# A layer whose activation transposes move from sixteen small VectorE operations to two wide VectorE operations and sixteen ScalarE copies

## The reference

```
u = rms_norm(h); z = u @ w_in               # four mixers on slices of z -> o_0..o_3
merged = sum_j sigmoid(z_merge_j) * (o_j @ w_branch[j])
h = h + merged @ w_out                      # 2048 x 2048
v = rms_norm(h)
h = h + square(relu(v @ w_up)) @ w_down     # w_up 2048 x 8192, w_down 8192 x 2048
h = h + sigmoid(h @ w_pg) * (p @ w_pp)      # 2048 x 2048
out = rms_norm(h)
```

## Time and profile before

| | us |
|---|---|
| median of 3 runs | 1621.71 (1620.98 to 1622.74) |
| the profiled execution | 1620.44 |
| its span, first to last instruction | 1618.7 |
| PE busy | 1594.5 |
| DVE busy | 1188.3 |
| ACT busy | 765.2 |

### The profile page before, as it was taken

How to read it: one execution, slowest core, us unless ns; L and a number is a source line. 1 busy time by engine, 2 the same in 40 slices (tenths; PEclk the granted TensorE clock), 3 DMA queues, 4 the chain that set the end, 5 groups by cost and what they waited for, 6 DMA issues and landing times.

```text
span 1618.7 us, 20043 instructions
## 1 busy us (share of the span) xinstructions
PE 1594.5 (99%) x7422; PEld 1305.8 (81%) x7422; DVE 1188.3 (73%) x1613; ACT 765.2 (47%) x898; POOL 0.7 (0%) x5
## 2 busy tenths in 40 slices
PE   9999999999999999999999999999999999999997
PEld 7888887778777788888878788887888788878886
DVE  6547847785988986887988845885569655888865
ACT  7444455656344454344464433453344434444455
POOL 0000000000000000000000000000000000000000
PEclk9999999999999999999999999999999999999999
DMA  9686656465666667876666566665665666655663
GB/s 326 192 290 202 184 182 182 143 181 164 208 196 182 210 207 250 284 240 235 199 182 194 192 192 192 188 200 187 192 188 186 197 192 193 187 193 182 220 198 127
DMA packets 163426, 325.32 MB, mean 201 GB/s; under 512 B 10640, under 2 KB 15888, under 8 KB 162448
## 3 DMA queue, kind: packets, MB, share of 16 engines
q1 hardware_dynamic: 163344, 324.23, 63.9%
HBM read 313.70 MB, written 10.49 MB: 200 GB/s over the span
## 4 chain that ended last, share of the span: by engine, by line
PE 91%; DVE 6%; ACT 1%; issue 1%; DMA 0%; ACTq 0%; SPq 0%
PE ps L374 29%; PE ps L375 29%; PE ps L376 29%; DVE ps L419 3%; DVE sb L357 2%; PE ps L791 1%; ACT sb L350 0%; ACT sb L1006 0%; DVE sb L405 0%; PE ps L666 0%; PE ps L719 0%; PE ps L702 0%; PE ps L390 0%; DVE sb L1412 0%; DMA sb<-in_w_mix 0%
## 5 line engine op out<-in xcount | busy, mean ns | idle before, releaser
L357 DVE TENSOR_TENSOR sb<-sb,sb 128x1024 fp32r<-128x1024 f32 x560 | 680.1, 1223 | 301.0 <-ACT sb L350 289.1
L350 ACT ACTIVATE sb<-sb 128x1024 fp32r<-128x1024 f32 x560 | 589.2, 1060 | 648.8 <-PE ps L376 626.6
L374 PE MATMUL ps<-sb,sb 128*128 128x512 f32 (+1 forms) x2224 | 869.9, 391 | 9.6 <-DVE sb L405 6.6
L375 PE MATMUL ps<-sb,sb 128*128 128x512 f32 (+1 forms) x2224 | 862.9, 388 | 0.0
L376 PE MATMUL ps<-sb,sb 128*128 128x512 f32 (+1 forms) x2224 | 862.7, 388 | 0.0
L374 PEld LDWEIGHTS ps<-sb,sb 128*128 128x128 f32 x2224 | 417.5, 188 | 103.4 <-issue 7.6
L376 PEld LDWEIGHTS ps<-sb,sb 128*128 128x128 f32 x2224 | 417.5, 188 | 86.9
L375 PEld LDWEIGHTS ps<-sb,sb 128*128 128x128 f32 x2224 | 417.7, 188 | 83.1
L419 DVE STREAM_TRANSPOSE ps<-sb 32x256 f32<-32x256 f32 x384 | 175.1, 456 | 6.4
L396 ACT ACTIVATE sb<-ps 128x1024 fp32r<-128x1024 f32 x26 | 26.6, 1025 | 64.6 <-DVE ps L419 64.6
L1672 DVE TENSOR_TENSOR sb<-sb 128x1024 f32<-128x1024 f32 x16 | 19.6, 1226 | 25.7 <-ACT sb L1113 25.7
(11 more groups left out here) (239 smaller groups left out, 483.2 us busy)
## 6 DMA issues: line engine op xcount, KB each, us to landing
sb<-in_w_in SPq DMA_DIRECT2D x128, 512.0 KB, 4.0
sb<-in_w_up SPq DMA_DIRECT2D x128, 512.0 KB, 3.9
sb<-in_w_down SPq DMA_DIRECT2D x128, 512.0 KB, 4.3
sb<-in_w_mix SPq DMA_DIRECT2D x64, 512.0 KB, 4.1
sb<-in_w_branch SPq DMA_DIRECT2D x32, 512.0 KB, 5.5
sb<-in_w_out SPq DMA_DIRECT2D x32, 512.0 KB, 4.5
sb<-in_w_pg SPq DMA_DIRECT2D x32, 512.0 KB, 3.7
gate_mem<-sb SPq DMA_DIRECT2D x16, 512.0 KB, 5.1
```

Source lines behind the costliest of these rows:

```text
L350: act.activation(whi[:, j % RING, :], raw[:, j % RING, :], ACT.Copy).then_inc(hi_done, 1)
L357: eng.tensor_tensor(wlo[:, j % RING, :], raw[:, j % RING, :], whi[:, j % RING, :].bitcast(F32), ALU.subtract).then_inc(lo_done, 1)
L374: pe.matmul(o, xh, w_h, start=first and k == 0, stop=False)
L375: pe.matmul(o, xh, w_l, start=False, stop=False)
```

## The change

`blocks` on DVE is replaced by two steps. `strips` on DVE takes two transposes, one for each token tile, over all 128 partitions and 512 elements: each 32x32 block is transposed and stays in its strip of 32 partitions. They write to `aux[1 - par]`, the other PSUM tensor, in step 0 of the group, right behind the split of that step. Then ACT makes the sixteen moves between strips as copies from `aux[1 - par]` to `aux[par]` in the new `blocks`, 32 partitions by 256 elements each, in steps 1 to 3 (`turned`), the first of which waits for the semaphore `strips_done`. `quad_hi` and `quad_lo` stay in step 4. The transposes of the mixers' quads on PE are not touched.

```diff
-        def blocks(v, par, src, lo, hi):
-
+        def strips(v, par, src):
+
+            for tt in range(TT):
+                dst = aux[1 - par][:, :].rearrange("p (r t k n) -> p t k r n", r=4, t=TT, k=4)[:, tt]
+                ins = v.transpose(dst, src(tt).rearrange("p (k r m) -> p k r m", k=4, r=4))
+            ins.then_inc(strips_done, 1)
+
+        def blocks(act, n, par, lo, hi):
+
+            if lo == 0:
+                act.wait_ge(strips_done, n + 1)
             for i in range(lo, hi):
                 q, r = i // 4, i % 4
                 dst = aux[par][32 * r:32 * r + 32, :].rearrange("p (k t m) -> p t k m", k=4, t=TT)[:, :, :, 32 * q:32 * q + 32]
-                ins = v.transpose(dst, src[32 * q:32 * q + 32, :, :, 32 * r:32 * r + 32])
+                src = aux[1 - par][32 * q:32 * q + 32, r * S:(r + 1) * S].rearrange("p (t k m) -> p t k m", t=TT, k=4)
+                ins = act.activation(dst, src, ACT.Copy)
             if hi == 16:
                 ins.then_inc(tp_in, 1)
...
+            def turned(j, n, par):
+
+                if 1 <= j <= 3:
+                    blocks(act, n, par, (0, 5, 10)[j - 1], (5, 10, 16)[j - 1])
+
...
                         split_hi(act, u, j + AHEAD)
+                        if first and n == 0:
+                            turned(j, NCH - 1, (TP_H + NCH - 1) % 2)
+                        if 1 <= n <= NCH:
+                            turned(j, g * NCH + (TP_FF - TP_H + n - 1), (TP_FF + n - 1) % 2)
...
-            def turn(j, par, src):
-
-                if 1 <= j <= 3:
-                    blocks(v, par, src, (0, 5, 10)[j - 1], (5, 10, 16)[j - 1])
...
+            def turn_h(k, tp):
+
+                strips(v, (tp + k) % 2, lambda tt: h[:, tt, k * C:(k + 1) * C])
...
-                        if 1 <= n <= NCH:
-                            if j == 1:
-                                v.wait_ge(sg["sq_done"], g * NCH + n)
-                            turn(j, (TP_FF + n - 1) % 2, relu[(n - 1) % 2].rearrange("p (t k f) -> p t k f", t=TT, k=4))
...
+                        if 1 <= n <= NCH and j == 0:
+                            v.wait_ge(sg["sq_done"], g * NCH + n)
+                            strips(v, (TP_FF + n - 1) % 2, lambda tt: relu[(n - 1) % 2][:, tt * C:(tt + 1) * C])
```

More of the change, by code:

```diff
@@ L272, in hybrid_layer @@
         tp_hi = sem("tp_hi")
+        strips_done = sem("strips_done")
         tp_lo = sem("tp_lo")
@@ L1085, in _ @@
                         merged_hi(NCH - 1)
+                    if n:
+                        turned(j, n - 1, (TP_H + n - 1) % 2)
                     if n and j == 4:
@@ L1093, in mlp_group @@
                         split_hi(act, u, j + AHEAD)
+                        if first and n == 0:
+                            turned(j, NCH - 1, (TP_H + NCH - 1) % 2)
+                        if 1 <= n <= NCH:
+                            turned(j, g * NCH + (TP_FF - TP_H + n - 1), (TP_FF + n - 1) % 2)
+                        if final and n > NCH:
+                            turned(j, TP_P - TP_H + n - NCH - 1, (TP_P + n - NCH - 1) % 2)
                         if j == 4 and 1 <= n <= NCH:
@@ L1131, in _ @@
                     split_hi(act, U_PG + n, j + AHEAD)
+                    if n == 0:
+                        turned(j, TP_P - TP_H + NCH - 1, (TP_P + NCH - 1) % 2)
                     if n == 0 and j == 4:
@@ L1608, in _ @@
                 v.sem_inc(sg["merged_done"], 1)
-            def turn(j, par, src):
-                if 1 <= j <= 3:
-                    blocks(v, par, src, (0, 5, 10)[j - 1], (5, 10, 16)[j - 1])
-            def turn_h(j, k, tp):
-                turn(j, (tp + k) % 2, h[:, :, k * C:(k + 1) * C].rearrange("p t (k f) -> p t k f", k=4))
+            def turn_h(k, tp):
+                strips(v, (tp + k) % 2, lambda tt: h[:, tt, k * C:(k + 1) * C])
             def add_residual(n, par):
@@ L1629, in _ @@
                         merged_lo(NCH - 1)
-                    if n and j == 1:
+                    if n and j == 0:
                         v.wait_ge(grp_free, 2 * (G_WO + n))
-                    if n:
-                        turn_h(j, n - 1, TP_H)
+                        turn_h(n - 1, TP_H)
                     if n and j == 4:
@@ L1645, in mlp_group @@
                         split_lo(v, u, j + AHEAD)
-                        if first and n == 0:
-                            if j == 1:
-                                v.wait_ge(grp_free, 2 * (G_WO + NCH))
-                            turn_h(j, NCH - 1, TP_H)
-                        if 1 <= n <= NCH:
-                            if j == 1:
-                                v.wait_ge(sg["sq_done"], g * NCH + n)
-                            turn(j, (TP_FF + n - 1) % 2, relu[(n - 1) % 2].rearrange("p (t k f) -> p t k f", t=TT, k=4))
[L1654 to L1657, removed]
+                        if first and n == 0 and j == 0:
+                            v.wait_ge(grp_free, 2 * (G_WO + NCH))
+                            turn_h(NCH - 1, TP_H)
+                        if 1 <= n <= NCH and j == 0:
+                            v.wait_ge(sg["sq_done"], g * NCH + n)
+                            strips(v, (TP_FF + n - 1) % 2, lambda tt: relu[(n - 1) % 2][:, tt * C:(tt + 1) * C])
+                        if final and n > NCH and j == 0:
+                            v.wait_ge(grp_free, 2 * (G_PG - NCH + n - NCH))
+                            turn_h(n - NCH - 1, TP_P)
                         if j == 4 and 1 <= n <= NCH:
@@ L1691, in _ @@
                     split_lo(v, U_PG + n, j + AHEAD)
-                    if n == 0 and j == 1:
+                    if n == 0 and j == 0:
                         v.wait_ge(grp_free, 2 * G_PG)
-                    if n == 0:
-                        turn_h(j, NCH - 1, TP_P)
+                        turn_h(NCH - 1, TP_P)
                     if n == 0 and j == 4:
```

## The result

| | before | after |
|---|---|---|
| median of 4 runs, us | 1621.35 (1620.57 to 1622.74) | 1611.05 (1610.59 to 1612.04) |
| span of the profiled execution, us | 1618.7 | 1609.2 |

What follows compares the result with a forecast made beforehand. PE, busy 1594.5 of 1618.7 us, was taken as the bound, so only its stalls could be won: 5 x 1.6 + 2.5 = 10.5 us, and 1621.7 - 10.5 = 1611.2 us, range 1610.0 to 1619.5.

Steps and rivals of the forecast that it cites:

- six stalls: PE's waits for quad_lo ahead of tile 6: five costing 1.6 us each and one 2.5, together 10.5 us.
- The likeliest case: All stalls gone, -10.5 us, giving 1611.2 us (1610.2 to 1612.2); chance 0.60.
- c: Step from one of ACT's sixteen strip copies to the next; taken as 0.28 us.
- step 6: Took 0.28 us a copy from the 0.26 row: sixteen take 4.5 us, quad done a microsecond ahead of its deadline.
- natural place: Earliest start of ACT's split of tile 7 that PE allows, 1091.51 us in the MLP quad; forecast about 0.7 behind it.
- the partial case: Copies not overlapping, c between 0.342 and 0.42: only part of the stalls won, gain 7.6 us, 1614.1 us; chance 0.18.
- steps 1 and 2: DVE's strip transposes: 0.72 us each if strips run in parallel, starting 1.25 behind the split of tile 3, ending at 1085.79.
- step 3: ACT's sixteen copies with splits of tiles 5 and 6 among them, 0.93 us a split, before the split of tile 7.
- step 4: Quad done 3.47 us behind the start of split 7, which must start by 1093.16, so sixteen copies may take 5.48 us.
- What costs nothing: The other 18 quads, asked for later, and ACT's added 107 us of 853 idle; PE's list, SP's and DMAs unchanged.
- the slower one: Copies of 0.5 us or more make ACT the bound, each further 0.01 us costing 1 us; 1627 us at 0.52; chance 0.09.

Runs made afterwards that it cites:

- extra_8: Changed kernel with eight more ScalarE copies, which nobody reads, behind the sixteen of each quad: 1637.69 us, ratio 1.0094.
- extra_3: Changed kernel with three more ScalarE copies, which nobody reads, behind the sixteen of each quad: 1618.06 us, ratio 0.9966.
- copies_stay: Changed kernel with each of the sixteen copies kept in its own strip of partitions, so blocks land in wrong places: 1610.7 us, one run.
- copies_in_halves: Changed kernel with each of the sixteen copies made as two of 128 elements, same strips read and written: 1615.9 us, one run.
- strips_late: Changed kernel with the two strip transposes one step later, behind the split of tile 4: 1622.66 us, ratio 0.9995.
- before_by_target: Kernel before with its sixteen VectorE transposes reordered, four sources for one target strip, then the next target: 1620.93 us, ratio 0.9992.

## Why the prediction was right

The forecast was 1611.2 us and all six stalls gone; measured 1611.05. Its account of the gain held: a ceiling of 10.5 us from six stalls (10.4 by the starts), none of it outside the six quads, and the deadline for the split of tile 7. The likeliest case came out, but with no room where a microsecond was forecast, and partly by luck; that is worth reading by its terms. Counted from the start of the relu in front of the group (1080.63 before, 1077.16 after), in us:

| | forecast | measured |
|---|---|---|
| strips end | 5.16 | 4.88 |
| from there to the split of tile 7 | 6.37 | 7.73 |
| split of tile 7 | 11.53 | 12.61 |
| latest without a stall | 12.53 | 12.5 to 12.6 |

- *The value of c* (step 6) was off: 0.28 taken, 0.36 measured. The row it was read from, 0.26 behind the mixer's copy, is of operations on all 128 partitions, and such copies do come 0.27 apart from PSUM to PSUM too; the sixteen change their strip at each copy. By the prediction's own sum c = 0.36 is past the limit of 0.342 and belongs to the partial case, 16 x 0.018 = 0.29 us of stall in each MLP group. So the mechanism of that rival, a copy that does not overlap its neighbour, is the one that was measured, and the reason for setting it aside (260.85 to 261.11) did not hold. The split of tile 7 came 1.7 us behind its natural place, where 0.7 was given.
- *Strips* (steps 1 and 2): 0.70 us each as forecast (0.72), which only the parallel case gives; it fits the 32x32 array per bank of which the Trainium skill, "VectorE: DVE Perf Modes", section "The three transpose paths", tells. But the two overlap (1.31 for the pair, not 1.46), and start 1.13 behind the split, not 1.25: the row for the 1.25 is of a transpose to another strip than the last one written. Together 0.28 us earlier, just what c had used up.
- *Copies* (step 3): a split among the copies takes 1.07 us where 0.93 was counted, since the copy behind it starts at another strip of PSUM than the copy in front of it; the split behind the last copy of a batch starts 0.28 behind it, as an overlapped one, where c was counted. The two nearly cancel.
- *Deadline* (step 4): right to 0.1 us. The delay that came was 0.06.
- *What costs nothing*: right. The eighteen other quads and DVE's relief moved the span by 0.7 us at most.
- *The rivals*: the slower one, ACT as the bound from 0.5 us a copy on, has the sign that `extra_8` gave, whose copies come to (5.6 + 3.1) / 16 = 0.54 us for each of the sixteen. Its price was too low: the rival's sum gives 1629 us at 0.54, and 1637.7 was measured, and among what it left out are the late starts of two groups and the slow matmuls.

So the middle of the forecast was right by errors of opposite sign, and that is luck. The range up to 1619.5 was not too wide: 1.25 us more on the chain, in `extra_3`, took back 6.8 of the 9.5 us.

The overlap of about 93 ns between ACTIVATEs that the Trainium skill gives ("ScalarE: Activation LUTs", section "What ACT_TABLE_LOAD costs") is near what copies show whose strips stay (on average 67 ns in `copies_stay` and 68 in `copies_in_halves`), and it is not there for the others; the measurement decides, and the sum by its figure, c = 0.306, would have been short by 0.05 us a copy.

## What to carry to other kernels

Where an engine is at 99%, list its waits first and price them by the starts of its own instructions: six stalls of a few us set both what could be won and which six of 24 quads to touch. Then write the deadline of the chain as a sum and ask how much room each engine leaves; a busy share of 56% on ACT said nothing about a chain with no time to spare. For small operations on 32 partitions, read the step between starts, not the duration, and take it from a row whose partitions change in the same way.

## What the runs showed of the hardware that was not expected

ScalarE copies on one strip of 32 partitions overlapped the next only where both strips stayed: 0.26 to 0.30 us from start to start against 0.33 to 0.37 for 256 elements, 0.17 against 0.24 for 128. The strip is compared with that of the last operation in the same memory, also across a split in between (0.95 against 1.07 us). On VectorE the narrow transposes, whose strips change, come 0.467 us apart and the wide ones 0.34; no run has narrow ones whose strips stay, but the first transpose behind a split comes at 1.14 or 1.26 us by the strip in front. A copy from PSUM took 351 ns to PSUM and 376 to SBUF.

A stall of PE can cost more than its length. In `strips_late` the wait of 2.17 us was followed by matmuls 0.43 us apart, and a window over them shows a granted clock of 0.50, the 1.2 GHz level, then 1.00 again:

```profile
834.90:837.90 3.00, 3.00 (x9) 2.32 (x8) 1.04 (x1) 2.88 (x4) 0.00 (x0) 0.50 0.01 4
838.50:841.50 3.00, 3.00 (x15) 2.46 (x14) 2.20 (x4) 2.68 (x4) 0.00 (x0) 1.00 0.67 186
```

(The columns are the window, its length, busy us and count of PE, PEld, DVE, ACT and POOL, the granted clock, the DMA share and GB/s.) It was the same after waits of 4.12, 3.04 and 3.78 us in `extra_8`, each followed by about eight matmuls at 0.43, some 1.6 us lost, and after one of 2.08 in `before_by_target`; but not after two of 3.12 us in `extra_8`, nor after the 2.21 us of the kernel before. So the length of the wait alone does not decide it, and what does is open.
